# Adding the experts' output to a token-major stream: one-hot places, token weight on VectorE, last norm by token

## The chip, the cores and the metric

The kernel runs on one core of a Trainium2 chip. The metric is device time in microseconds (us) of one execution, median of several. Lower is better. In what follows PE is TensorE (matmuls), DVE is VectorE, ACT is ScalarE, POOL is GpSimd, SP is the engine whose queue issues nearly all loads.

## What is computed

One inference step of a two-layer backbone over 128 context tokens and 128 latent tokens, model width 1024, all in fp32. Each layer: a modulated RMS norm, attention and a pooling mixer, a gated residual; then a modulated RMS norm and a feed-forward part, dense in layer 0 and top-2-of-8 experts in layer 1, with a gated residual. A last RMS norm gives the two outputs. The change lies in the experts' part of layer 1 and in the last norm:

```
gates = sum(one_hot(top_i, 8) * softmax(top_v)[..., None], axis=1)
y = 0
for e in range(8):
    y = y + gates[:, e:e + 1] * swiglu(x, we_gate[e], we_up[e], we_down[e])
x = x + g2 * y                      # g2: one gate vector for the context tokens, one for the latents
out = x * rsqrt(mean(x * x) + EPS) * final_norm_g
```

## The kernel before

Five engines run programs written by hand, each in its own order, tied by semaphores. The residual stream is `xT`: channels on the 128 partitions (8 groups `k`), the 256 tokens (`b` = 0 context, 1 latents) along the free axis. The weights (466 MB in all) stream through a ring of slots that SP fills; a slot is filled again when the matmuls that read it have been counted in `pieces_used`.

**Routing.** After the last norm of layer 1, PE computes the router's logits (L1531), turns the normed activations to `h2` with tokens on partitions (L1535), and DVE picks the top two and each token's place among the tokens of its expert. `place` (L1148, L1152) writes two matrices for each expert: `P`, one-hot (token to one of CAP = 96 places), and `Pg`, the same with the token's weight in it. `gather(e)` (L1553) multiplies `h2` by `P` and gives `xg`, the expert's tokens with channels on partitions. PE transposes all `Pg` (L1586) to `PgT` before the first expert; ACT and DVE copy it out of PSUM.

**An expert.** Its 3584 hidden columns come in four steps. `gate_up` (L1610) multiplies the tokens with the gate and up weights; ACT applies silu (L845, L846), DVE multiplies (`hm`, L1203, L1204), PE transposes the result (`turn`, L1622), ACT and DVE copy it (`hT_first`, `hT_last`), and `down` (L1636) accumulates the expert's output in PSUM banks 3 to 5. Down matmuls of one step are interleaved with gate and up matmuls of the next. The expert's output leaves PSUM while the next expert's first step runs: ACT copies the even half to `Y` (`take_Y`), DVE adds the odd half (`add_Y`, L1177, L1182).

**The seam.** So at the end of each expert's first gate/up step PE does, in this order, the last expert's `combine` (L1565, eight products of `Y` and `PgT`, 256 columns each, in fp32, into banks 3, 4, 5 and 0), `turn(0)`, and then waits for `acc_ready`: DVE adds the four banks into an accumulator `acc` (`add_up`, L1189) that lies in the buffer called `sq`. The first matmul of step 1 writes where these results stood, so it comes behind the fourth addition. On DVE the two `hm` products of step 0 stand ahead of the four additions. The place is called the seam below; there are eight. At the first one PE and DVE add zeros.

```
                        if i + 1 == GATE_UP_END[0]:
                            pe.wait_ge(Y_ready, k + (rnd + 1))
                            combine(e, k * NSTEP + 1)
                            turn(0)
                            pe.wait_ge(acc_ready, k * 4 + (4 * rnd + 4))
```

**The end.** Every expert gathers for the next one before its last down matmuls, the eighth too, though nothing uses that. Then come `add_Y`, `combine` and `add_up` for the last expert, a register load and a branch (a second round of experts that these inputs don't need), 16 gated residual updates of `xT` on DVE (`residual`, L960), squares on ACT (L669), 16 sums over channels by one-column matmuls (L1265), root and reciprocal, a broadcast by matmul (L1273), eight scaled products on DVE (L909), 16 transposes (L1680), four copies and two stores of 512 KB.

Of the kernel before, what the change touches and what calls it, by code (L numbers as in the profile page):

```python
# [18 lines left out]
D = 1024  # L19
T = 128  # L20
DEPTH = 2
# [12 lines left out]
NE = 8  # L34
FE = 3584
EPS = 1e-6
# [29 lines left out]
        (0, 1, 0, 4, 0), (0, 1, 1, 4, 1), (1, 0, 2, 4, 2), (1, 0, 1, 4, 3),  # L66
        (1, 0, 0, 5, 0), (1, 1, 1, 5, 1), (1, 1, 2, 5, 2), (1, 1, 0, 5, 3))
TURN_BANK, GATHER_BANK = 6, 0
COMBINE_BANKS = (3, 4, 5, 0)
# [190 lines left out]
def program(nc, ins, consts, y_prompt, y_sample, new_ckv, new_kpe):  # L260
# [10 lines left out]
    with ctx:  # L271
# [35 lines left out]
        oh = sb("oh", 128, 4, 2, NE)  # L307
        over = sb("over", 128, 1, dt=i32)
# [54 lines left out]
        P = sb("P", 128, NE + 1, 2, CAP)  # L363
        PgT = sb("PgT", 128, NE + 1, 2, 128)
        Y = sb("Y", 128, D)
        xg = sb("xg", 128, KD, CAP)
        hT_first = sb("hT_first", 128, 4, 128)
        hT_last = sb("hT_last", 128, 4, 64)
        sg_at = place_at[0]
        sg = sb("sg", 128, 2, 512)  # L370
        hm = sb("hm", 128, 2, 512)

        place_at[0] = sg_at
        Pg = sb("Pg", 128, NE, 2, CAP)
        place_at[0] = sg_at + 4 * 2048
        yout = h2[:, :, :].rearrange("p b d -> p (b d)")
        acc = sq
# [26 lines left out]
        P_ready, Pg_ready, PgT_done, PgT_first_ready, PgT_last_ready = (sem(x) for x in ("P_ready", "Pg_ready", "PgT_done", "PgT_first_ready", "PgT_last_ready"))  # L404
        moe_zero, over_ready, shift_ready = sem("moe_zero"), sem("over_ready"), sem("shift_ready")
        esg_ready, eh_ready, ehT_done, ehT_first_ready, ehT_last_ready = (sem(x) for x in ("esg_ready", "eh_ready", "ehT_done", "ehT_first_ready", "ehT_last_ready"))
        Y_even_ready, Y_moved, Y_ready, cmb_done, acc_ready = sem("Y_even_ready"), sem("Y_moved"), sem("Y_ready"), sem("cmb_done"), sem("acc_ready")
        gat_done, xg_first_ready, xg_last_ready = sem("gat_done"), sem("xg_first_ready"), sem("xg_last_ready")
        outT_done, y_first_ready, y_second_ready = (sem(x) for x in ("outT_done", "y_first_ready", "y_second_ready"))
# [69 lines left out]
        def _(sp):  # L479
# [100 lines left out]
            sp.wait_ge(y_first_ready, 1)  # L580
            sp.wait_ge(y_second_ready, 1)
            sp.dma_start(y_prompt, yout[:, 0:D]).then_inc(stored, 16)
            sp.wait_ge(y_first_ready, 2)
            sp.wait_ge(y_second_ready, 2)
            sp.dma_start(y_sample, yout[:, D:2 * D]).then_inc(stored, 16)
# [5 lines left out]
        def _(pool):  # L591
# [40 lines left out]
        def _(act):  # L632
# [73 lines left out]
            def mixer(l):  # L706
# [75 lines left out]
                for m in gap[1:2]:  # L782
                    take_rows(m)
# [46 lines left out]
            def experts(rnd):  # L830
# [22 lines left out]
                with act.Fori(0, NE) as e:  # L853
                    expert(e)
# [853 lines left out]
```

## Time and profile before

| | |
|---|---|
| median of three runs | 1539.85 us (1538.51 to 1541.7) |
| the profiled execution | 1541.1 us |
| its span, first to last instruction | 1538.9 us |
| PE busy | 1467.5 us, 95% of the span |
| DVE busy | 365.6 us, 24% |
| ACT busy | 268.8 us, 17% |
| read from HBM | 462.80 MB, 302 GB/s over the span |
| mean granted clock of PE | 0.968 of 2.4 GHz |

The profiled execution's time is its span and 2.2 us around it. A busy share is an average over stages: the eight experts take about 120.7 us each, from about 538 us on, and what an engine's wait is worth there is read in one expert and counted eight times. The tail begins at 1504 us, when the last down matmul ends. The granted clock has two levels, 1.0 (2.4 GHz) and 0.5 (1.2 GHz); a value between is a mean over a stretch.

### The profile page before, as it was taken

The numbers are of one execution on the slowest core, as the hardware profiler recorded it, in microseconds if no ns is written. First come the engines' busy times: TensorE is split into PE (matmuls) and PEld (weight loads), VectorE is DVE, ScalarE is ACT, GpSimd is POOL, SyncE is SP. The second block draws the span as 40 slices with busy tenths as digits, with TensorE's granted clock in tenths as the row PEclk, the third lists the DMA queues.
The fourth block names the chain that finished last, engine by engine and source line by source line (L and its number), as shares of the span: only waits on it lengthen the run. The fifth ranks groups of instructions, "written<-read, shape, count | busy, mean of one in ns | idle before, by whom it ended". The sixth has DMA issues, their size and how long they took to land.

```text
span 1538.9 us, 29578 instructions
## 1 busy us (share of the span) xinstructions
PE 1467.5 (95%) x13084; PEld 798.5 (52%) x13084; DVE 365.6 (24%) x647; ACT 268.8 (17%) x434; POOL 30.9 (2%) x63
## 2 busy tenths in 40 slices
PE   5898999999998799999999999999999999999995
PEld 3857799998857733433343343343343343343344
DVE  2434555454433420020020011011011011002004
ACT  3323544443332300000000000000000000010001
POOL 0020000000020000000000000000000000000000
PEclk9899899998999699999999999999999999999997
DMA  9668877553663889989999999999999999999910
GB/s 346 223 226 297 290 263 249 188 181 124 222 226 114 328 294 393 385 323 378 396 347 357 394 351 354 391 353 347 398 354 345 391 361 346 386 364 351 378 73 29
DMA packets 164779, 466.05 MB, mean 303 GB/s; under 512 B 12810, under 2 KB 55476, under 8 KB 150324
## 3 DMA queue, kind: packets, MB, share of 16 engines
q1 hardware_dynamic: 162756, 462.81, 81.1%
q8 instruction: 104, 1.70, 0.4%
q10 hardware_dynamic: 1904, 1.41, 0.3%
q14 instruction: 15, 0.12, 0.0%
HBM read 462.80 MB, written 1.38 MB: 302 GB/s over the span
## 4 chain that ended last, share of the span: by engine, by line
PE 90%; DVE 4%; issue 2%; ACT 2%; SPq 1%; DMA 1%; DVEq 0%; ACTq 0%
PE ps L1610 38%; PE ps L1636 19%; PE ps L1326 5%; PE ps L1328 5%; PE ps L1327 5%; PE ps L1287 2%; PE ps L1553 2%; PE ps L1337 2%; PE ps L1622 2%; PE ps L1265 1%; PE ps L1499 1%; PE ps L1501 1%; PE ps L1500 1%; DVE sq L1189 1%; DMA ring<-in_w_ada 1%
## 5 line engine op out<-in xcount | busy, mean ns | idle before, releaser
L1610 PE MATMUL ps<-ering,xg 128*32 128x512 f32 (+1 forms) x6144 | 596.9, 539 | 4.9 <-DVE sq L1189 3.5
L1610 PEld LDWEIGHTS ps<-ering,xg 128*32 128x32 f32 x6144 | 198.4, 110 | 383.6 <-issue 347.6
L1636 PE MATMUL ps<-ering,hT_first 128*32 128x512 f32 x1792 | 307.6, 593 | 0.0
L1326 PE MATMUL ps<-hx,high 128*128 128x256 f32 x640 | 183.0, 286 | 16.8 <-DVE low L885 13.2
L1203 DVE TENSOR_TENSOR hm<-sg,ps 128x512 f32<-128x512 f32 (+1 forms) x32 | 19.9, 621 | 742.4 <-ACT sg L846 742.4
L1327 PE MATMUL ps<-hx,high 128*128 128x256 f32 x640 | 181.1, 283 | 0.0
L1328 PE MATMUL ps<-hx,low 128*128 128x256 f32 x640 | 181.0, 283 | 0.0
L1636 PEld LDWEIGHTS ps<-ering,hT_first 128*32 128x32 f32 x1792 | 82.1, 110 | 183.3 <-issue 177.1
L1636 PE MATMUL ps<-ering,hT_last 128*32 128x512 f32 x896 | 153.7, 592 | 0.0
L845 ACT ACTIVATE sg<-ps 128x512 f32<-128x512 f32 (+1 forms) x32 | 17.4, 544 | 748.0 <-PE ps L1610 748.0
L885 DVE TENSOR_TENSOR low<-ring,high 128x1024 fp32r<-128x1024 f32 x102 | 121.9, 1223 | 95.8 <-ACT high L653 95.8
L1326 PEld LDWEIGHTS ps<-hx,high 128*128 128x128 f32 x640 | 123.0, 192 | 21.5 <-DVE low L885 14.6
L1328 PEld LDWEIGHTS ps<-hx,low 128*128 128x128 f32 x640 | 123.0, 192 | 0.0
L1327 PEld LDWEIGHTS ps<-hx,high 128*128 128x128 f32 x640 | 122.6, 192 | 0.0
L653 ACT ACTIVATE high<-ring 128x1024 fp32r<-128x1024 f32 x102 | 104.3, 1055 | 73.8 <-PE ps L1328 39.9
L1287 PE MATMUL ps<-ring,silu_c 128*32 128x512 f32 x384 | 53.2, 680 | 0.1
L1499 PE MATMUL ps<-fx,high 128*128 128x256 f32 x176 | 49.5, 281 | 0.0
L1500 PE MATMUL ps<-fx,high 128*128 128x256 f32 x176 | 49.1, 279 | 0.0
L1501 PE MATMUL ps<-fx,low 128*128 128x256 f32 x176 | 49.1, 279 | 0.0
L1565 PE MATMUL ps<-PgT,Y 96*128 96x256 f32 x144 | 36.9, 413 | 6.2 <-DVE Y L1182 6.2
L1622 PEld LDWEIGHTS ps<-cst,hm 128*128 128x128 f32 x224 | 29.9, 207 | 22.3 <-DVE hm L1204 21.9
L1636 PEld LDWEIGHTS ps<-ering,hT_last 128*32 128x32 f32 x896 | 40.7, 110 | 0.0
(195 smaller groups left out, 942.9 us busy)
## 6 DMA issues: line engine op xcount, KB each, us to landing
ering<-in_moe_w_gate SPq DMA_DIRECT2D x224, 512.0 KB, 5.1
ering<-in_moe_w_up SPq DMA_DIRECT2D x224, 512.0 KB, 6.5
ering<-in_moe_w_down SPq DMA_DIRECT2D x112, 1024.0 KB, 7.2
ring<-in_w_ada SPq DMA_DIRECT2D x48, 1024.0 KB, 7.1
ring<-in_ffn_w_gate SPq DMA_DIRECT2D x11, 1024.0 KB, 5.6
ring<-in_ffn_w_up SPq DMA_DIRECT2D x11, 1024.0 KB, 7.4
ring<-in_ffn_w_down SPq DMA_DIRECT2D x11, 1024.0 KB, 5.5
ring<-in_w_in SPq DMA_DIRECT2D x8, 1024.0 KB, 9.4
```

The lines of the kernel that those rows point to most:

```text
L653: A(next(halves(q, raw)), raw, ACT.Copy).then_inc(high_ready, 1)
L885: V.tensor_tensor(lo, raw, hi, ALU.subtract).then_inc(low_ready, 1)
L1287: last = mm(mod_rows_of(m)[32 * i:32 * i + 32, :], silu_c[:, k, :], w[:, i, :], start=half == 0, stop=half == 1)
L1326: mm(out, hi[:, k, :], xh, start=n == 0, stop=False)
L1327: mm(out, hi[:, k, :], xl, start=False, stop=False)
L1328: last = mm(out, lo[:, k, :], xh, start=False, stop=n == KD - 1)
L1499: mm(o, hi[:, 0, mc], xh, start=a, stop=False, skip_group_check=True)
L1500: mm(o, hi[:, 0, mc], xl, start=False, stop=False, skip_group_check=True)
L1501: last = mm(o, lo[:, 0, mc], xh, start=False, stop=z, skip_group_check=True)
L1610: last = mm(ps[32 * group:32 * group + 32, bank, 0:width], xg[:, kk, 32 * g:32 * g + 32], w[:, t, r, c * width:(c + 1) * width], start=kk ...
L1622: last = nc.tensor.transpose(ps[:, TURN_BANK + part, n * 128:(n + 1) * 128], hm[:, part, a:a + 255:2], ident)
L1636: last = mm(ps[32 * group:32 * group + 32, bank, :], h, w[:, odd, 512 * half:512 * (half + 1)], start=(s, i) == (0, 0), stop=(s, i) == (NS ...
```

## The change

- **Stream.** Before layer 1's router PE transposes `xT` (between the sums of the norm, in `norm(3)`) and ACT and DVE copy it to `xt`, tokens on partitions. PE also broadcasts the gate vector g2 over all partitions (16 products of a broadcast column with the identity) into `gate`, which takes the place of `xT`.
- **Places.** Only the one-hot `P` is made. It is transposed to `PT` not before the first expert but in the middle of its first gate/up step (`turn_places`). The weights go to `w_slot`.
- **Output.** `take_Y` and `add_Y` keep the expert's output in `Y` and split it in `Yh` (rounded to the one-pass format `f32r`) and `Yl` (the rest). `combine` is now eight products of 512 columns, places times `Yh` and places times `Yl`, one pass each, four banks of tokens x channels.
- **Adding.** `add_up` takes two DVE instructions for each bank: `scalar_tensor_tensor` (PSUM times the token's weight times `gate`) into `gated`, then an addition to `xt` that waits for the first. PE waits for the fourth `gated_ready`.
- **First and last.** The first expert has no `add_Y`, `combine` or `add_up`; the last has no `gather`.
- **End.** `combine` for the last expert works half by half as `Yh` and `Yl` come. The norm is done with tokens on partitions: ACT squares and sums rows of `xt` in one instruction, then root, reciprocal and one product with `fin` (the last norm's gain, loaded over all partitions by a DMA on ACT's queue in the routing stage). No matmul of the norm and no transposes are left.

```diff
+COMBINE = ((0, 0, 3), (0, 1, 4), (1, 0, 5), (1, 1, 0))
+COMBINE_END = ((0, 0, 0), (0, 1, 1), (1, 0, 2), (1, 1, 6))
...
@@ gpsimd
             pool.wait_ge(h2T_done, 1)
-            nc.gpsimd.memset(P[:, NE, :, :], 0.0)
-            nc.gpsimd.memset(PgT[:, 0, :, :], 0.0)
-            nc.gpsimd.memset(hm[:, 1, :], 0.0)
-            nc.gpsimd.memset(acc[:, :, :], 0.0).then_inc(moe_zero, 1)
+            nc.gpsimd.memset(hm[:, 1, :], 0.0).then_inc(moe_zero, 1)
@@ scalar
+            act.dma_start(fin[:, :], ins["final_norm_g"].rearrange("(o n) -> o n", o=1).to_broadcast([128, D])).then_inc(fin_in, 16)
...
+            def take_Y(n, even=Y_even_ready, added=Y_ready, high_half=Yh_ready):
+
+
+                A(Y[0:CAP, 0:512], ps[0:CAP, 3, :], ACT.Copy).then_inc(even, 1)
+                A(Y[64:CAP, 512:1024], ps[96:128, 3, :], ACT.Copy).then_inc(even, 1)
+                A(Y[0:64, 512:1024], ps[0:64, 5, :], ACT.Copy).then_inc(even, 1)
+                for half in range(2):
+                    act.wait_ge(added, 2 * n - 1 + half)
+                    A(Yh[0:CAP, 512 * half:512 * (half + 1)], Y[0:CAP, 512 * half:512 * (half + 1)], ACT.Copy).then_inc(high_half, 1)
...
+            take_Y(1, Y_even_end, Y_end, Yh_end)
 
             for b in range(2):
-                A(yout[:, b * D:b * D + 512], ps[:, 1 + 2 * b, :], ACT.Copy).then_inc(y_first_ready, 1)
+                for half in range(2):
+                    act.wait_ge(xt_end, 2 * b + half + 1)
+                    A(squared_x[:, half, :], xt[:, b, 512 * half:512 * (half + 1)], ACT.Square,
+                      accum_out=stat[:, 2 * b + half:2 * b + half + 1]).then_inc(yss_ready, 1)
+                act.wait_ge(yrt_ready, 2 * b + 1)
+                A(rt[:, b:b + 1], rt[:, b:b + 1], ACT.Sqrt, scale=1.0 / D).then_inc(yrt_ready, 1)
@@ vector
-            def add_up(done):
-                for r, bank in enumerate(COMBINE_BANKS):
-                    dve.wait_ge(cmb_done, done + (r + 1))
-                    a = acc[:, 2 * r:2 * r + 2, :]
-                    V.tensor_tensor(a, a, ps[:, bank, :].rearrange("p (k t) -> p k t", k=2), ALU.add).then_inc(acc_ready, 1)
+            def add_Y(e, n, even=Y_even_ready, added=Y_ready, high_half=Yh_ready, low_half=Yl_ready, now=now_ready):
+
+
+                places = PT[0:CAP, e, :, :] if isinstance(e, int) else PT[0:CAP, bass.ds(e, 1), :, :].rearrange("p o b t -> p (o b) t")
+                V.tensor_copy(PT_now[0:CAP, :, :], places).then_inc(now, 1)
+
+                def odd(a, z, half, bank, at):
+                    y = Y[a:z, 512 * half:512 * (half + 1)]
+                    return V.tensor_tensor(y, ps[at:at + z - a, bank, :], y, ALU.add)
+
+                def low_of(half):
+                    x = slice(512 * half, 512 * (half + 1))
+                    dve.wait_ge(high_half, 2 * n - 1 + half)
+                    V.tensor_tensor(Yl[0:CAP, x], Y[0:CAP, x], Yh[0:CAP, x], ALU.subtract).then_inc(low_half, 1)
+
+                dve.wait_ge(even, 3 * n - 2)
+                odd(0, CAP, 0, 4, 0).then_inc(added, 1)
+                dve.wait_ge(even, 3 * n - 1)
+                odd(64, CAP, 1, 4, 96)
+                low_of(0)
+                dve.wait_ge(even, 3 * n)
+                odd(0, 64, 1, 5, 64).then_inc(added, 1)
+                low_of(1)
+
+            def add_up(e, n, combined=cmb_done, weighted=gated_ready, summed=xt_added, places=COMBINE):
+
+
+                for r, (b, half, bank) in enumerate(places):
+                    x = slice(512 * half, 512 * (half + 1))
+                    w = w_slot[:, b, e:e + 1] if isinstance(e, int) else w_slot[:, b, bass.ds(e, 1)]
+                    dve.wait_ge(combined, 4 * n - 3 + r)
+                    V.scalar_tensor_tensor(gated[:, r % 2, :], ps[:, bank, :], w, gate[:, b, x], ALU.mult, ALU.mult).then_inc(weighted, 1)
+                    dve.wait_ge(weighted, 4 * n - 3 + r)
+                    V.tensor_tensor(xt[:, b, x], xt[:, b, x], gated[:, r % 2, :], ALU.add).then_inc(summed, 1)
...
@@ tensor
+                    if t == 2 * DEPTH - 1:
+                        for b in range(2):
+                            last = nc.tensor.transpose(ps[:, X_BANK[b, k // 4], k % 4 * 128:(k % 4 + 1) * 128], xT[:, k, b * T:(b + 1) * T], ident)
...
             mixer(1)
+
+            pe.wait_ge(mod_ready, DEPTH * ADA_ITEMS)
+            for i, ((b, half), bank) in enumerate(GATE_BANK.items()):
+                if bank == 0:
+                    pe.wait_ge(normed, 2 * (2 * DEPTH - 1) + 2)
+                for k in range(4 * half, 4 * half + 4):
+                    row = mod[:, 1, 40 + k, b:b + 1].to_broadcast([128, 128])
+                    last = mm(ps[:, bank, k % 4 * 128:(k % 4 + 1) * 128], row, ident, start=True, stop=True)
+                if i % 2:
+                    last.then_inc(gate_done, 1)
...
+                for r, (b, half, bank) in enumerate(places):
+                    if hidden is not None and bank == 0:
                         pe.wait_ge(eh_ready, hidden)
+                    for part, (y, ready) in enumerate(zip((Yh, Yl), halves_of_Y)):
+                        pe.wait_ge(ready, 2 * n - 1 + half)
+                        last = mm(ps[:, bank, :], PT_now[0:CAP, b, :], y[0:CAP, 512 * half:512 * (half + 1)], start=part == 0, stop=part == 1)
+                    last.then_inc(combined, 1)
...
+                        if begins and i + 1 == GATE_UP_END[0] // 2:
+                            turn_places()
                         if i + 1 == GATE_UP_END[0]:
-                            pe.wait_ge(Y_ready, k + (rnd + 1))
-                            combine(e, k * NSTEP + 1)
+                            if begins:
+                                pe.wait_ge(PT_first_ready, rnd + 1)
+                                pe.wait_ge(PT_last_ready, rnd + 1)
+                            else:
+                                combine(k, k * NSTEP + 1)
                             turn(0)
-                            pe.wait_ge(acc_ready, k * 4 + (4 * rnd + 4))
+                            if not begins:
+                                pe.wait_ge(gated_ready, 4 * k)
                         elif what == "d" and s < NSTEP - 1 and j == 2 * E_WIDTH[s] // 256 - 1:
                             turn(s + 1)
-                            if s + 1 == NSTEP - 1:
+                            if s + 1 == NSTEP - 1 and not ends:
                                 gather(e + 1)
```

DVE at the seam, before: the two `hm` products, the first of four like additions into `acc` (`sq`), and the copy of the transposed hidden values behind them.

```order
L1203 TENSOR_TENSOR hm<-sg,ps 128x512 [waits esg_ready]
L1204 TENSOR_TENSOR hm<-sg,ps 64x512
L1187 REGISTER_ALU
L1189 TENSOR_TENSOR sq<-sq,ps 128x512 [waits cmb_done]
...
L1207 REGISTER_ALU
L1209 COPY hT_last<-ps 128x256 [waits ehT_done]
```

The same place now, with two of the four pairs (`sq` is where `gated` lies, `xT` where `gate` lies):

```order
L1267 TENSOR_TENSOR hm<-sg,ps 128x512 [waits esg_ready]
L1268 TENSOR_TENSOR hm<-sg,ps 64x512
L1246 SCALAR_TENSOR_TENSOR sq<-ps,w_slot,xT 128x512 [waits cmb_done]
L1248 TENSOR_TENSOR xt<-xt,sq 128x512 [waits gated_ready]
L1246 SCALAR_TENSOR_TENSOR sq<-ps,w_slot,xT 128x512 [waits cmb_done]
L1248 TENSOR_TENSOR xt<-xt,sq 128x512 [waits gated_ready]
...
L1273 COPY hT_last<-ps 128x256 [waits ehT_done]
```

Between the `hm` products and the fourth `gated_ready`, for which PE waits, four instructions have become seven, three of them behind a wait for the one ahead.

DVE in the tail, before, from the last `add_Y` on:

```order
L1182 TENSOR_TENSOR Y<-ps,Y 32x512 [waits Y_moved]
L1182 TENSOR_TENSOR Y<-ps,Y 32x512 x5
L1189 TENSOR_TENSOR sq<-sq,ps 128x512 [waits cmb_done] x4
L1221 UNCONDITIONAL_BRANCH [waits acc_ready]
L960 SCALAR_TENSOR_TENSOR xT<-sq,mod,xT 128x128 x16
L900 TENSOR_SCALAR rt<-ps 128x2 [waits ss_done,x_ready]
L902 RECIPROCAL rt<-rt 128x2 [waits rt_ready]
L909 SCALAR_TENSOR_TENSOR sq<-xT,vecT,ps 128x256 [waits rs_done]
L909 SCALAR_TENSOR_TENSOR sq<-xT,vecT,ps 128x256 x7
```

And now, `add_Y` and the first of the four pairs of `add_up`, and behind these the end for one of the two halves of the tokens:

```order
L1223 TENSOR_TENSOR Y<-ps,Y 96x512 [waits Y_even_end]
L1223 TENSOR_TENSOR Y<-ps,Y 32x512 [waits Y_even_end]
L1228 TENSOR_TENSOR Yl<-Y,Yh 96x512 [waits Yh_end]
L1223 TENSOR_TENSOR Y<-ps,Y 64x512 [waits Y_even_end]
L1228 TENSOR_TENSOR Yl<-Y,Yh 96x512 [waits Yh_end]
L1246 SCALAR_TENSOR_TENSOR sq<-ps,w_slot,xT 128x512 [waits cmb_end]
L1248 TENSOR_TENSOR xt<-xt,sq 128x512 [waits gated_end]
...
L1293 TENSOR_SCALAR rt<-stat 128x1 [waits yss_ready,fin_in]
L1295 RECIPROCAL rt<-rt 128x1 [waits yrt_ready]
L1297 SCALAR_TENSOR_TENSOR h_77<-xt,rt,fin 128x1024 [waits yrs_ready]
```

The 16 residual updates, the eight scaled products and the copies have gone from the tail; the branch now stands ahead of `add_Y`.

## Rows read from the trace of the kernel before

**Rows 1.** The page, part 5, whole span

```profile
L885 DVE TENSOR_TENSOR low<-ring,high 128x1024 fp32r<-128x1024 f32 x102 | 121.9, 1223 | 95.8 <-ACT high L653 95.8
```

**Rows 2.** Windows, one expert: stretch, length, busy by engine, granted clock, DMA, GB/s

```profile
1021.68:1142.40 120.72, 120.20 (x1185) 45.65 (x1180) 14.31 (x24) 7.59 (x15) 0.00 (x0) 1.00 0.96 366
```

**Rows 3.** Timeline of PE, one seam; columns: start, length, instructions [idle before]

```profile
1042.21 3.82 PE L1565 MATMUL ps<-PgT,Y 96*128 96x256 f32 x16
1045.87 1.11 PE L1622 MATMUL ps<-cst,hm 128*128 128x128 f32 x8
1047.41 5.36 PE L1610 MATMUL ps<-ering,xg 128*32 128x512 f32 x48 [0.44 <-DVE sq L1189]
```

**Rows 4.** Timeline of DVE, the same seam

```profile
1044.16 0.69 DVE L1204 TENSOR_TENSOR hm<-sg,ps 64x512 f32<-64x512 f32 x1
1044.88 2.48 DVE L1189 TENSOR_TENSOR sq<-sq,ps 128x512 f32<-128x512 f32 x4
```

**Rows 5.** Groups of DVE by shape, 500 to 1539: busy us, mean ns, idle before

```profile
L1189 DVE TENSOR_TENSOR sq<-sq,ps 128x512 f32<-128x512 f32 x36 | 22.6, 683 | 4.6 <-PE ps L1565 4.4
...
L960 DVE SCALAR_TENSOR_TENSOR xT<-sq,mod,xT 128x128 f32<-128x128 f32 x16 | 4.3, 344 | 1.2 <-issue 1.2
...
L909 DVE SCALAR_TENSOR_TENSOR sq<-xT,vecT,ps 128x256 f32<-128x256 f32 x8 | 3.2, 476 | 1.3 <-PE ps L1273 1.3
```

**Rows 6.** Timeline, all engines, from the last gather to the end

```profile
1495.55 3.71 PE L1553 MATMUL ps<-P,h 128*128 128x96 f32 x32
...
1504.62 0.59 ACT L827 ACTIVATE Y<-ps 96x512 f32<-96x512 f32 x1 [4.83 <-PE ps L1636]
...
1505.72 0.70 DVE L1177 COPY Y<-ps 32x512 f32<-32x512 f32 x1 [5.86 <-ACT Y L828]
1506.45 4.20 DVE L1182 TENSOR_TENSOR Y<-ps,Y 32x512 f32<-32x512 f32 x6
...
1510.70 6.34 PE L1565 MATMUL ps<-PgT,Y 96*128 96x256 f32 x16 [6.15 <-DVE Y L1182]
...
1518.97 4.29 DVE L960 SCALAR_TENSOR_TENSOR xT<-sq,mod,xT 128x128 f32<-128x128 f32 x16 [1.19 <-issue]
1520.14 0.63 ACT L669 ACTIVATE sq<-xT 128x512 f32<-128x512 f32 x1 [14.45 <-DVE xT L960]
...
1520.82 6.99 PE L1265 MATMUL ps<-ones,sq 128*128 128x1 f32 x32 [3.78 <-ACT sq L669]
...
1530.37 3.28 PE L1680 MATMUL ps<-cst,sq 128*128 128x128 f32 x16 [0.58 <-DVE sq L909]
...
1535.06 0.34 SPq L585 DMA_DIRECT2D out<-h  x1
```

**Rows 7.** Windows, tail and first gather; after POOL's column: the granted clock

```profile
1509.00:1510.00 1.00, 0.00 (x0) 0.00 (x0) 0.97 (x3) 0.00 (x0) 0.00 (x0) 0.61 0.00 0
...
1516.00:1517.00 1.00, 1.00 (x5) 0.59 (x3) 0.69 (x1) 0.00 (x0) 0.00 (x0) 0.98 0.00 0
...
1519.00:1520.00 1.00, 0.00 (x0) 0.00 (x0) 1.00 (x4) 0.00 (x0) 0.00 (x0) 0.73 0.03 8
...
1533.00:1534.00 1.00, 0.65 (x5) 0.41 (x4) 0.36 (x2) 0.31 (x1) 0.00 (x0) 0.94 0.00 0
...
528.50:534.50 6.00, 5.92 (x32) 5.78 (x32) 6.00 (x30) 0.01 (x1) 0.00 (x0) 0.62 1.02 412
```

**Rows 8.** Timeline, routing stage and start of the first expert

```profile
514.55 7.00 PE L1531 MATMUL ps<-wr,sq 128*128 128x8 f32 x32 [4.62 <-DVE sq L922]
...
528.54 5.92 PE L1553 MATMUL ps<-P,h 128*128 128x96 f32 x32 [1.55 <-DVE P L1148]
530.82 3.92 DVE L1152 TENSOR_SCALAR Pg<-cst,oh 128x96 f32<-128x96 f32 x16
...
535.25 1.95 PE L1586 MATMUL ps<-cst,Pg 128*96 128x128 f32 x16 [0.79 <-DVE over L1166]
...
538.62 20.81 PE L1610 MATMUL ps<-ering,xg 128*32 128x512 f32 x192 [1.42 <-ACT PgT L835]
```

More of the change, by code:

```diff
@@ L783, in mixer @@
                     take_rows(m)
+                if l:
+                    act.wait_ge(xt_done, 1)
+                    for b, half in ((0, 0), (1, 0), (0, 1)):
+                        A(xt[:, b, 512 * half:512 * (half + 1)], ps[:, X_BANK[b, half], :], ACT.Copy).then_inc(xt_first_ready, 1)
                 norm_b(2 * l + 1, l == 0)
@@ L806, in _ @@
             mixer(1)
+            act.wait_ge(gate_done, 2)
+            for b, half in ((0, 0), (1, 1)):
+                A(gate[:, b, 512 * half:512 * (half + 1)], ps[:, GATE_BANK[b, half], :], ACT.Copy).then_inc(gate_first_ready, 1)
             act.wait_ge(top2_ready, 1)
@@ L1191, in experts @@
             def experts(rnd):
+                if rnd:
+                    add_Y(NE, NE * rnd)
+                    add_up(NE, NE * rnd)
                 place(rnd)
@@ L1204, in expert @@
                         V.tensor_tensor(hm[0:64, 1, 0:width], sg[0:64, 1, 0:width], ps[64:128, 2, 0:width], ALU.mult).then_inc(eh_ready, 1)
-                        if s == 0:
-                            add_up(k * 4 + 4 * rnd)
+                        if s == 0 and not begins:
+                            add_up(e, k)
                         dve.wait_ge(ehT_done, k * NSTEP + (s + 1))
@@ L1209, in expert @@
                         V.tensor_copy(hT_last[:, 0:n, :], ps[:, TURN_BANK + 1, 0:width].rearrange("p (n t) -> p n t", n=n)[:, :, 0:64]).then_inc(ehT_last_ready, 1)
-                    take_xg(k + (rnd + 2))
-                with dve.Fori(0, NE) as e:
+                    if not ends:
+                        take_xg(k + 2)
+                expert(0, begins=True)
+                with dve.Fori(1, NE - 1) as e:
                     expert(e)
-                add_Y(9 * (rnd + 1))
-                add_up(36 * rnd + 32)
-                dve.wait_ge(acc_ready, 36 * (rnd + 1))
+                expert(NE - 1, ends=True)
             experts(0)
@@ L1673, in _ @@
                     experts(rnd)
-            norm(2 * DEPTH)
-            spread(2 * DEPTH)
-            for k in range(KD):
-                pe.wait_ge(h_ready, 2 * DEPTH + k + 1)
-                for b in range(2):
-                    last = nc.tensor.transpose(ps[:, 1 + 2 * b + k // 4, (k % 4) * 128:(k % 4 + 1) * 128], hT[:, k, b * T:(b + 1) * T], ident)
-            last.then_inc(outT_done, 1)
+            combine(1, None, now_end, (Yh_end, Yl_end), cmb_end, COMBINE_END)
 OVER_LIMIT = float(CAP)
```

198 lines of the change are left out of this document (107 added, 91 removed).

## Prediction

> **What bounds the kernel now.** I read one expert by windows first [rows 2]: PE is busy 120.20 of 120.72 us at the full clock, so almost all that an expert costs is PE's own work. The loads are not the bound: at 366 GB/s no matmul waits for them there, while the same queues gave 412 GB/s in the first gather [rows 7]. So PE time at the seam and in the tail counts in full, and longer DVE work counts where PE waits for it. The seam decides that [rows 3, 4]. PE begins `combine` at 1042.21 and gate/up of step 1 at 1047.41, that is 5.20 us, with a wait of 0.44 us for L1189 at the end. DVE starts the second `hm` product at 1044.16, ends it at 1044.85, and its four additions end at 1047.36: PE goes on 0.05 us later. So the seam ends by DVE today, and combine and turn lie beside it. The tail [rows 6] runs from the last down matmul (1504.55, by ACT's start) to 1538.9, 34.35 us, in a chain that goes from engine to engine.
>
> **The seam, seven times.** The cheaper `combine` (two passes for each bank in place of four) shortens PE work that DVE's chain covers, and is worth nothing. DVE's chain gets longer. One `scalar_tensor_tensor` takes 344 ns for 128 elements and 476 for 256 [rows 5], 132 for each 128 more, so 740 for 512. The addition of two SBUF tensors: L885 takes 1223 ns for 1024 [rows 1], less 533 (512 elements at the slope that these lengths give) is 690. The wait between the two costs what the wait between L1177 and L1182 does: start to start 0.73 for 0.70, so 0.03 [rows 6]. Behind an instruction that it needn't wait for, the next one starts early: four L1189 in 2.48 at 0.683 each [rows 4, 5] is a pitch of 0.60, 0.08 less than the length. A pair is then 0.74 + 0.03 + 0.69 - 0.08 = 1.38. The fourth `gated_ready` comes 3 x 1.38 + 0.74 = 4.88 us after 1044.88 where 2.48 stood: **+2.40 a seam, +16.8 for seven**. The `hT_last` copy queues behind it by 0.7 more, but its reader, `down`, comes two gate/up groups (5.36 in all [rows 3]) later. The copies to `PT_now`, `Yh` and `Yl` lie under the 20 us of gate/up. Bounds for a seam: -0.99 (DVE hidden, PE alone: `hm` end at 2.64, 0.43 for two products, 1.11 for the turn, 4.2 in all) and +2.9.
>
> The Trainium skill (VectorE: DVE Perf Modes, The DRAIN you can't avoid) says that the next instruction doesn't start before the pipe is empty and that a semaphore adds nothing. Here four additions overlap by 0.08 each. By that rule a pair would be 1.43 and the sum 1 us higher.
>
> **The clock at the seam.** This is the term I am least sure of. Now PE is without work from the end of `turn(0)` (1042.21 + 2.67 + 0.43 + 1.11 = 1046.4) to 1049.8: 3.4 us, and 1.4 us ahead of the fourth bank's products. In the tail the clock fell to half when PE had been idle from 1517.04 to 1519.46 (0.73 in that microsecond), 2.4 us, and another time only after 4.7 us, at 1509.2 [rows 6, 7]. 3.4 lies between. It rose after 4.6 us of gather (0.62 over 6 us from 528.5), after 5.3 us of `combine` (1510.70 to 1516.0), and 2.7 us after the transposes began at 1530.37 (0.94 in 1533 to 1534) [rows 6 to 8]. Work at half the clock loses half its time: 1.35 to 2.65, middle 2.0. Gate/up fills PE at the full clock [rows 2], so that loss is on the path. The first seam has an idle stretch of 2.7 too. I take seven of eight: **+14**; bounds 0 and 8 x 2.65 = 21.
>
> The Trainium skill (TensorE: Matmul & The Clock Gate, Part 4: PE-mode transpose) says that transposes don't count as work for the clock. Here it rose while PE did little but transposes [rows 6, 7]. By that rule the turn would count as idle, the gap would be 4.5, all eight seams would fall, and the sum would be 2 higher.
>
> **Start of the experts.** PE goes from the end of the gather (534.46) to gate/up at 538.62, 4.16 us, because Pg (3.92), its transposes (1.95) and the copies stand between [rows 8]. Now only the `xg` copy does, 0.6: -3.55. The 16 transposes come inside gate/up, 1.95 and about 0.25 for breaking the stream: +2.2. Ahead of it: 14 of 16 transposes at 0.12 in the norm delay its sums, at most 1.7. The 16 gate products lie in PE's 4.62 us idle stretch ahead of the router [rows 8] when the clock is full (16 x 0.22 = 3.5), and end up to 3 late at half clock; dense work there brings the clock up for part of the router's 7.0, which is at half (about 0.22 for each of 32, 0.12 at full). The `xt` and `gate` copies and POOL's shorter memsets cost nothing, hidden by the router; if the router were gone they would cost 2. The `fin` DMA delays ACT's `h2` copies by some 0.45, which the wait for P (1.55 [rows 8]) covers. I take -1.5 for it all, bounds -4 and +3. Together **-2.85**.
>
> **First seam.** Without `combine` and `add_up` it ends 2.64 + 0.05 + 1.11 = 3.8 after gate/up for 5.2: **-1.35**.
>
> **Last gather.** 3.71 us of PE [rows 6] go; the `hT` copies, so far beside it, show with 0.5: **-3.0** (bounds -3.6 and -2.5).
>
> **The tail**, from down's end as 0: three ACT copies (0.59 each, pitch 0.49) and the first odd addition, `Yh` at 2.2, `Yl` at 2.9, the other odd half 3.6, `Yh` 4.3, `Yl` 5.0 (ACT 0.63 in SBUF, DVE 0.69). Four pairs of 1.38 from 5.0: 10.6. Products are covered by these. Sum 0.16, root 0.20, reciprocal 0.17 with 0.03 between each, and a product of 1024 (0.74 + 0.53 = 1.27): the first half's output at 12.6. ACT squares the second half meanwhile (0.63 twice and the sum's read), and with the same steps it stands at 14.5. The last store: issue at 1535.06 to 1538.9 is 3.84 for two stores that share the queues; one alone of 512 KB at the 412 GB/s of [rows 7] is some 0.8 less, 3.1. End at 17.6 for 34.35: **-16.75** (bounds -18.5 and -14). Register load and branch, 1.19 ahead of L960 [rows 6], are hidden by the last down matmuls.
>
> **Sum.** +16.8 + 14 - 2.85 - 1.35 - 3.0 - 16.75 = +6.85. On the profiled execution's 1541.1 this is 1547.95. The median of the runs shown is 1.25 below that execution, so **1546.7**, +0.44%.
>
> **Rivals.**
> - *The clock stays up at the seams.* The stretch of 3.4 us is shorter than the 4.7 that it once took. Then the sum is -7.15: 1532.7, faster. Against it: the fall after 2.4. It decides as soon as the clock takes less than 7 us in all. Chance 0.16.
> - *It falls in about half of them, or rises soon*: +7, so 1539.7, no change. 0.20.
> - *It falls in all eight and stays down 5.3 us of work*: +21, so 1553.7. The Trainium skill's rule on transposes would lead here. 0.10.
> - *The change does what it says and DVE's pairs are covered*: -0.99 x 7, no clock loss, sum -31, 1509. It would need the pairs to fit in 1.5 us; nothing in the rows says so. 0.02.
> - *Forecast*, 1541 to 1551: 0.52.
>
> **Numbers.** 0.2% (3.1 us) is about what a measurement of this kernel can tell from no change. Faster: rival one, the fourth, and a little of the second, 0.19. Within: most of the second and the forecast's low end, 0.19. Slower: 0.62. The range for 8 in 10, 1534 to 1552, leaves out half of the first rival, the fourth and the upper half of the third; the likeliest case alone is 1541 to 1551.
>
> **What would show it.** Right: PE's wait at L1700 for `gated_ready` 3 us or more, seven times; the seam 7.6 us; a granted clock below 1.00 in expert windows, and an expert of 123 to 126 us. The tail from down's end to the end 17 to 19 us. Wrong: an expert of 123.1 with the clock at 1.00 (first rival); pairs on DVE shorter than 1.3; the gather ending later than 536, if the gate products are late.

## The result and the profile after

The changed kernel takes 1547.61 us (median of 8 runs, 1545.38 to 1550.56), the kernel before 1540.37 (8 runs, 1532.24 to 1544.3). The ratio is 1.0058, 95% interval 1.0042 to 1.0073: slower by 0.6%. The profiled execution of the changed kernel took 1548.21 us, its span is 1546.4, 7.5 more than before, and its mean granted clock 0.963 for 0.968.

The page of the changed kernel, first row of part 1, and the group of gate/up in part 5 (busy us, mean ns, idle time ahead and what ended most of it), with the same group of the kernel before behind it:

```profile
PE 1452.6 (94%) x12968; PEld 766.0 (50%) x12968; DVE 363.5 (24%) x624; ACT 283.7 (18%) x463; POOL 28.7 (2%) x60
...
L1700 PE MATMUL ps<-ering,xg 128*32 128x512 f32 (+1 forms) x6144 | 613.7, 551 | 23.5 <-DVE sq L1246 22.8
```

```profile
L1610 PE MATMUL ps<-ering,xg 128*32 128x512 f32 (+1 forms) x6144 | 596.9, 539 | 4.9 <-DVE sq L1189 3.5
```

PE is busy 15 us less than before in a span that is 7.5 us longer, so it is idle for 22.4 us more, and the group says behind what: DVE's L1246. The same 6144 gate/up matmuls are also busy for 613.7 us where they were for 596.9. The waits of PE from 500 us on (total us, times, longest):

```profile
PE ps L1700 <- DVE sq L1246: 22.8, 7, 3.3
PE ps L1654 <- DVE hm L1268: 7.2, 7, 1.0
...
PE ps L1712 <- DVE hm L1268: 2.8, 1, 2.8
```

Seven waits of 3.26 us at the seams are new; before, a seam had 0.44 [rows 3]. Two experts by windows (columns as in [rows 2]):

```profile
1029.52:1153.97 124.45, 120.06 (x1176) 43.68 (x1172) 16.16 (x27) 9.45 (x18) 0.00 (x0) 0.99 0.93 355
903.50:1029.52 126.02, 121.63 (x1177) 43.93 (x1172) 16.16 (x27) 9.44 (x18) 0.00 (x0) 0.97 0.92 351
```

An expert took 120.72 [rows 2]. Now it takes 124.45 or 126.02, and the clock is no longer 1.00. One seam on PE:

```profile
1050.05 0.50 PE L1654 MATMUL ps<-Yh,PT_now 96*128 96x512 f32 x1
...
1052.74 0.50 PE L1654 MATMUL ps<-Yh,PT_now 96*128 96x512 f32 x1 [1.04 <-DVE hm L1268]
...
1053.31 1.11 PE L1712 MATMUL ps<-cst,hm 128*128 128x128 f32 x8
1057.68 6.65 PE L1700 MATMUL ps<-ering,xg 128*32 128x512 f32 x48 [3.26 <-DVE sq L1246]
```

and on DVE:

```profile
1052.71 0.75 DVE L1246 SCALAR_TENSOR_TENSOR sq<-ps,w_slot,xT 128x512 f32<-128x512 f32 x1
1053.50 0.69 DVE L1248 TENSOR_TENSOR xt<-xt,sq 128x512 f32<-128x512 f32 x1
1054.11 0.74 DVE L1246 SCALAR_TENSOR_TENSOR sq<-ps,w_slot,xT 128x512 f32<-128x512 f32 x1
...
1056.88 0.74 DVE L1246 SCALAR_TENSOR_TENSOR sq<-ps,w_slot,xT 128x512 f32<-128x512 f32 x1
```

The fourth product ends at 1057.62, and PE goes on 0.06 later. From the first combine product (1050.05) to step 1 it is 7.63 us; before, 5.20. DVE's pairs follow each other at 1.39 (three pairs in 4.17, from 1052.71 to 1056.88).

Then the clock. These are the 48 gate/up matmuls that follow each of the eight seams (length, PE, weight loads, granted clock, DMA share, GB/s):

```profile
557.29:563.09 5.80, 5.80 (x48) 1.48 (x48) 0.89 0.24 54
681.07:687.94 6.87, 6.87 (x48) 1.81 (x48) 0.75 0.17 52
805.92:813.69 7.77, 7.77 (x48) 1.85 (x48) 0.66 0.15 44
931.67:939.71 8.04, 8.04 (x48) 1.86 (x48) 0.64 0.18 49
1057.68:1064.16 6.48, 6.48 (x48) 1.61 (x48) 0.79 0.15 42
1182.14:1189.54 7.40, 7.40 (x48) 1.78 (x48) 0.70 0.15 34
1307.50:1315.36 7.86, 7.86 (x48) 1.86 (x48) 0.65 0.16 42
1433.34:1441.43 8.09, 8.09 (x48) 1.86 (x48) 0.64 0.22 59
```

At the full clock such a stretch takes 5.17 (below, in the third experiment). The seven later ones are longer by 1.70, 2.60, 2.87, 1.31, 2.23, 2.69 and 2.92, in all 16.3 us; the first by 0.63.

The start of the experts on PE:

```profile
508.52 3.76 PE L1604 MATMUL ps<-cst,mod 128*128 128x128 f32 x32
513.31 3.74 PE L1614 MATMUL ps<-wr,sq 128*128 128x8 f32 x32 [1.02 <-DVE sq L958]
...
522.94 6.13 PE L1640 MATMUL ps<-P,h 128*128 128x96 f32 x32 [1.13 <-DVE P L1192]
529.77 10.51 PE L1700 MATMUL ps<-ering,xg 128*32 128x512 f32 x96 [0.70 <-ACT xg L845]
540.21 1.95 PE L1677 MATMUL ps<-cst,P 128*96 128x128 f32 x16
```

The router takes 3.74 for 7.00, and gate/up begins at 529.77 for 538.62 [rows 8]. The tail, all engines:

```profile
1528.34 0.59 ACT L850 ACTIVATE Y<-ps 96x512 f32<-96x512 f32 x1 [5.51 <-PE ps L1726]
...
1533.54 0.75 DVE L1246 SCALAR_TENSOR_TENSOR sq<-ps,w_slot,xT 128x512 f32<-128x512 f32 x1
...
1537.18 1.28 ACT L904 ACT_TABLE_LOAD   x1
...
1539.77 1.28 DVE L1297 SCALAR_TENSOR_TENSOR h<-xt,rt,fin 128x1024 f32<-128x1024 f32 x1
...
1541.65 1.28 DVE L1297 SCALAR_TENSOR_TENSOR h<-xt,rt,fin 128x1024 f32<-128x1024 f32 x1
```

It runs from 1528.28, the last down matmul's end, to 1546.4: 18.12 us for 34.35.

Both profiled executions, stage by stage:

| stage | before | after | difference |
|---|---|---|---|
| to the first sum of layer 1's second norm | 503.20 | 502.29 | -0.9 |
| from there to the first gate/up | 35.42 | 27.48 | -7.9 |
| turn of the places inside gate/up | 0 | 2.02 | +2.0 |
| first seam (last gate/up matmul to step 1) | 5.71 | 5.28 | -0.4 |
| seven seams, by the same measure | 7 x 5.72 | 7 x 8.16 | +17.1 |
| low clock behind eight seams | 0 | 16.95 | +16.95 |
| last expert from step 1 to the end of down, without the low clock's part | 94.98 | 92.02 | -3.0 |
| tail | 34.35 | 18.12 | -16.2 |
| sum | | | +7.6 |

The first row is partly chance: the part of the kernel up to that sum took 494.4 to 505.0 us in the fourteen profiles of this document, and these two executions happen to lie 0.9 apart.

### The profile page after: what moved, and what is told of

It reads as the page before. It is cut to its first block, busy times and chain, and to the rows that moved or that the text cites. A ratio compares the mean times of both kernels' runs of the same rounds, so it can differ in the third digit from the quotient of the medians.

```text
span 1546.4 us, 29377 instructions
## 1 busy us (share of the span) xinstructions
PE 1452.6 (94%) x12968; PEld 766.0 (50%) x12968; DVE 363.5 (24%) x624; ACT 283.7 (18%) x463; POOL 28.7 (2%) x60
## 3 DMA queue, kind: packets, MB, share of 16 engines
HBM read 463.33 MB, written 1.38 MB: 301 GB/s over the span
## 4 chain that ended last, share of the span: by engine, by line
PE 89%; DVE 6%; ACT 2%; issue 2%; DMA 0%; SPq 0%; DVEq 0%; ACTq 0%
PE ps L1700 39%; PE ps L1726 18%; PE ps L1399 5%; PE ps L1401 5%; PE ps L1400 5%; PE ps L1360 2%; PE ps L1640 2%; PE ps L1410 2%; PE ps L1712 2%; DVE sq L1246 2%; PE ps L1572 1%; PE ps L1574 1%; PE ps L1573 1%; PE ps L1332 1%; PE ps L1370 1%
## 5 line engine op out<-in xcount | busy, mean ns | idle before, releaser
L1700 PE MATMUL ps<-ering,xg 128*32 128x512 f32 (+1 forms) x6144 | 613.7, 551 | 23.5 <-DVE sq L1246 22.8
L1712 PE MATMUL ps<-cst,hm 128*128 128x128 f32 x224 | 35.3, 299 | 3.6 <-DVE hm L1268 2.8
```

What stands on the lines that cost most here:

```text
L1700: last = mm(ps[32 * group:32 * group + 32, bank, 0:width], xg[:, kk, 32 * g:32 * g + 32], w[:, t, r, c * width:(c + 1) * width], start=kk ...
L1712: last = nc.tensor.transpose(ps[:, TURN_BANK + part, n * 128:(n + 1) * 128], hm[:, part, a:a + 255:2], ident)
```

## Experiments

The two theories: (A) the seam costs twice, by DVE's longer chain and by the clock, which falls because PE waits; (B) the long gate/up stretches behind the seams have another cause than the wait (late weights, the shorter combine, the turn). Each kernel is timed against the kernel before on one chip; the chip differs between some of the runs, and a difference of two medians from two chips is uncertain by a few us.

**Idle products in the wait.** Between the turn and the wait for `gated_ready` stand products that nobody reads:

```diff
                             if not begins:
+                                for _ in range(14):
+                                    mm(ps[:, 1, :], PT_now[0:CAP, 0, :], Yh[0:CAP, 0:512], start=True, stop=True)
                                 pe.wait_ge(gated_ready, 4 * k)
```

> The changed kernel with 14 extra one-pass products (places times Yh, into bank 1, which step 1 overwrites) between the turn and the wait at each of the seven later seams; DVE's work is untouched. They take about 3.0 us of the 3.26 us that PE waits there. My theory (waiting and the clock are two costs, and the second is about 2.3 us a seam): the seam stays at 7.6 us, the granted clock stays at 1.00 through seven experts, the first gate/up group goes from 6.6 to 8.3 us back to 5.36, and the time falls by about 16, from 1547.6 to 1531 to 1532. Rival (the long first groups have another cause, such as weights that come late): the time stays within 2 us of the changed kernel or grows.

1529.08 us, ratio to before 0.9928 (0.9903 to 0.9952). A seam of this kernel:

```profile
1050.46 1.11 PE L1712 MATMUL ps<-cst,hm 128*128 128x128 f32 x8
1051.32 3.44 PE L1747 MATMUL ps<-Yh,PT_now 96*128 96x512 f32 x14
1054.84 5.36 PE L1700 MATMUL ps<-ering,xg 128*32 128x512 f32 x48
```

The seam is as long as ever (8.16), the wait is filled, and none of the seven stretches behind it is longer than 5.18. The seven stretches give 16.3 us back, the median 18.5 (against that of the first measurement, on another chip). The two profiled executions lie only 12.0 apart (1536.25 and 1548.21), because this one reached the first gate/up 2.85 us later and lost 1.47 more behind the first seam, where nothing was changed. So the clock's part is about what the rows said. The order of the loads, DVE's work, the turn and the length of the seam are what they were, and the long stretches are gone: late weights or the turn did not make them, PE's idle time did. Theory A stands; whether the shorter combine has a part is the question of the long combine below.

**Bank 0 first.** DVE's order is changed, and PE's wait is split:

```diff
-                for r, (b, half, bank) in enumerate(places):
+                order = (3, 0, 1, 2) if places == COMBINE else (0, 1, 2, 3)
+                for r, i in enumerate(order):
+                    b, half, bank = places[i]
...
@@ down
                         if i == 0:
+                            if s == 0 and not begins:
+                                pe.wait_ge(gated_ready, 4 * k)
...
@@ seam
-                                pe.wait_ge(gated_ready, 4 * k)
+                                pe.wait_ge(gated_ready, 4 * k - 3)
```

> The changed kernel with DVE taking bank 0 first in add_up (order 0, 3, 4, 5), PE waiting for the first product only before gate/up of step 1, and for the fourth before the first down product, two gate/up groups later. My theory: PE waits for bank 0 alone, the seam is PE's own turn plus a short wait, 4.2 to 4.6 us for 7.6, the clock does not fall there, and the time falls by 7 x 3.2 + 16 = 38, to about 1509 to 1513. Rival 1 (the clock falls whatever the wait, because the turn and the hm wait alone are enough): 1524 to 1527. Rival 2 (DVE's chain, which still takes 5.5 us, makes the hT_last copy late for the first down product): a new wait of 1 to 2 us a seam at that product, 1517 to 1525.

1505.31 us, ratio 0.9777 (0.9755 to 0.9798). The seam on PE:

```profile
1032.12 0.50 PE L1656 MATMUL ps<-Yh,PT_now 96*128 96x512 f32 x1 [1.04 <-DVE hm L1270]
...
1032.70 1.11 PE L1714 MATMUL ps<-cst,hm 128*128 128x128 f32 x8
1033.82 5.36 PE L1702 MATMUL ps<-ering,xg 128*32 128x512 f32 x48
```

From 1029.43, the first combine product, to 1033.82 it is 4.39 for 7.63. Step 1 follows the turn without a wait. The clock stays at 1.00 through the seven experts. Only bank 0 is written by step 1; banks 3 to 5 are needed by `down`, two gate/up groups later. There DVE's longer queue shows a little:

```profile
1037.19 0.74 DVE L1248 SCALAR_TENSOR_TENSOR sq<-ps,w_slot,xT 128x512 f32<-128x512 f32 x1
...
1038.58 0.42 DVE L1275 COPY hT_last<-ps 128x256 f32<-128x256 f32 x1
1039.14 1.45 PE L1730 MATMUL ps<-ering,hT_first 128*32 128x512 f32 x9
```

The fourth product ends at 1037.93, but the `hT_last` copy only at 1039.00, and the first down matmul begins 0.14 behind it, 5.32 after step 1 for 5.17. So rival 1 of this run is out, and rival 2 is right in kind: it costs 0.15 a seam, 1 us in all, where it named 1 to 2 a seam. The time is 4 us below the range that I gave; a second measurement below lies in it.

**Four products first**, then the four additions, with four buffers for `gated`:

```diff
-                    dve.wait_ge(weighted, 4 * n - 3 + r)
-                    V.tensor_tensor(xt[:, b, x], xt[:, b, x], gated[:, r % 2, :], ALU.add).then_inc(summed, 1)
+                for r, (b, half, bank) in enumerate(places):
+                    dve.wait_ge(weighted, 4 * n - 3 + r)
+                    V.tensor_tensor(xt[:, b, x], xt[:, b, x], gated[:, r, :], ALU.add).then_inc(summed, 1)
```

> The changed kernel with the four scalar_tensor_tensor of a seam first, in four buffers, and the four additions behind them; PE waits for the fourth product as before. My theory: the fourth product comes 4 x 0.66 after the hm products, the seam is 5.2 to 5.5 us, PE is idle only 1.2 us ahead of step 1, the clock stays up, and the time falls by 7 x 2.2 + 16 = 31, to about 1516 (1513 to 1520). Rival (the clock falls at a wait of any length there): 1532. Rival 2 (the DVE queue as a whole sets the seam, not the fourth product): no change.

1516.81 us, ratio 0.9859 (0.9834 to 0.9885). DVE at a seam:

```profile
1034.59 2.73 DVE L1247 SCALAR_TENSOR_TENSOR sq<-ps,w_slot,xT 128x512 f32<-128x512 f32 x4
1037.23 2.49 DVE L1255 TENSOR_TENSOR xt<-xt,sq 128x512 f32<-128x512 f32 x4
```

The time lies in the range that I gave. The fourth product ends 2.73 after the first begins, the seam is 5.97 for 8.16 by the table's measure, and PE's wait ahead of step 1 is 1.07. I expected the clock to stay up. It did at five of seven seams, and fell at two. One stretch of 48 gate/up matmuls of each kind:

```profile
672.92:678.09 5.17, 5.17 (x48) 1.46 (x48) 1.00 0.25 63
1037.37:1044.24 6.87, 6.87 (x48) 1.81 (x48) 0.75 0.23 60
```

**Six idle products** where the first run had 14:

> The changed kernel with 6 extra products at the seam for the 14 of the earlier run: 1.3 us of the 3.26 us are filled, about 2.0 us stay idle. The seam stays at 7.6 us. In the kernel with its four scalar_tensor_tensor first, 1.07 us of idle time there let the clock fall at 2 of 7 seams. My theory (each idle microsecond raises the number of seams at which the clock falls): 2 to 5 of seven fall, 1534 to 1542. Rival (any filling keeps the clock up): 1531.

1534.66 us, ratio 0.9961 (0.9943 to 0.9979). The wait is 1.88, and the clock fell at two of seven seams, with 3.4 us in all. By the sums of the stretches it should stand 16.3 - 3.4 = 12.9 below the changed kernel: 1534.7. That the median meets this to 0.1 is chance, since the stretches are of one execution (it took 1538.35) and the medians of two chips.

**A combine as long as before.** The first product of each bank is made three times:

```diff
+                        if part == 0 and places == COMBINE:
+                            for _ in range(2):
+                                mm(ps[:, bank, :], PT_now[0:CAP, b, :], y[0:CAP, 512 * half:512 * (half + 1)], start=True, stop=True)
```

> The changed kernel with the first of the two products of each bank made three times over, so that PE has 16 passes in combine, as in the kernel before, for 8; DVE's work and all waits are untouched, and PE is still idle for about 2.8 us of the 3.26 us before step 1. My theory (the idle stretch itself brings the clock down): it still falls in most of the seven seams, and the time is 0 to 6 us below the changed kernel, 1542 to 1548. Rival (the clock falls because combine became short, the wait alone would not do it): all seven first gate/up groups back at 5.36, 1531 to 1533.

1540.89 us, ratio 1.0007 (0.999 to 1.0025). The wait ahead of step 1 is 2.74, and the wait for `hm` within combine is gone. The clock fell at five of seven seams, with 9.4 us in all, and the time lies 1.1 below the range that I gave and far above the rival's. So the wait alone does bring the clock down. The long combine takes 1.03 + 0.52 us of idle time away and puts work there; which of the two saved the clock at the other two seams, this run can't tell. The kernels in one table (idle time ahead of step 1 and ahead of the fourth bank's products, and the seven stretches, from one profile of each):

| kernel | wait ahead of step 1 | wait for `hm` within combine | long stretches of 7 | us lost in them | median |
|---|---|---|---|---|---|
| changed | 3.26 | 1.03 | 7 | 16.3 | 1547.6 |
| long combine | 2.74 | 0 | 5 | 9.4 | 1540.9 |
| 6 products | 1.88 | 1.03 | 2 | 3.4 | 1534.7 |
| four products first | 1.07 | 1.03 | 2 | 3.3 | 1516.8 |
| 14 products | 0.07 | 1.03 | 0 | 0 | 1529.1 |
| bank 0 first | 0 to 0.03 | 1.03 | 0 | 0 | 1505.3 |

**The kernel before with bank 0 first**, by a like edit to its own additions:

```diff
-                for r, bank in enumerate(COMBINE_BANKS):
+                for r in (3, 0, 1, 2):
+                    bank = COMBINE_BANKS[r]
...
-                            pe.wait_ge(acc_ready, k * 4 + (4 * rnd + 4))
+                            pe.wait_ge(acc_ready, k * 4 + (4 * rnd + 1))
```

> The kernel before with the same order of banks as the fast version of the changed kernel: DVE adds bank 0 first, PE waits for that addition before step 1 and for all four before the first down product. My theory (before, PE's own combine and turn are nearly as long as the seam): hm ends at 2.64, two products of the fourth bank 0.95, turn 1.11, so 4.7 us for 5.2, eight times 0.5: 4 us below the kernel before. Then most of the 33 us between the kernel before and that fast version come from the change once its wait is gone, and not from the order. Rival (the order alone gives the gain): 1515 or less.

1536.38 us, ratio 0.9988 (0.9973 to 1.0002). That doesn't part from no change by its time. Its profile shows the gain that was expected: the seam is 5.21 by the table's measure for 5.72, and the experts take 961.81 for 965.93, 4.1 less. But this edit changes the order in the tail as well, which the edit to the changed kernel leaves alone (`places == COMBINE`), and there it costs. The tail before, and now:

```profile
1510.70 6.34 PE L1565 MATMUL ps<-PgT,Y 96*128 96x256 f32 x16 [6.15 <-DVE Y L1182]
1512.82 0.69 DVE L1189 TENSOR_TENSOR sq<-sq,ps 128x512 f32<-128x512 f32 x1 [2.17 <-PE ps L1565]
...
1517.09 0.69 DVE L1189 TENSOR_TENSOR sq<-sq,ps 128x512 f32<-128x512 f32 x1 [0.18 <-PE ps L1565]
```

```profile
1498.12 7.06 PE L1566 MATMUL ps<-PgT,Y 96*128 96x256 f32 x16 [6.15 <-DVE Y L1182]
...
1505.22 2.48 DVE L1190 TENSOR_TENSOR sq<-sq,ps 128x512 f32<-128x512 f32 x4 [7.15 <-PE ps L1566]
```

All four additions now stand behind the fourth bank's products. From combine's start to the last addition's end it is 9.58 for 7.08, 2.5 more, of which combine itself has 0.7. So the time holds 4.1 us of gain at the seams and some 2 us of loss in the tail. At the seams the order alone is worth 4 us to the kernel before; behind the change it is worth about 40.

**The start: 16 idle products ahead of the router, in the kernel before.**

```diff
+            for i in range(16):
+                mm(ps[:, 7, i % 4 * 128:(i % 4 + 1) * 128], mod[:, 1, 40 + i % 8, 0:1].to_broadcast([128, 128]), ident, start=True, stop=True)
             pe.wait_ge(h_ready, 4)
```

> The kernel before with 16 idle products of 128 columns (a broadcast column times the identity, into a bank nobody reads) where PE waits for the activations ahead of the router; nothing else changed. My theory (the start gained about 8 us instead of 2.85 because the gate products keep PE's clock up, so that router, turn and gather run at full speed): router 3.8 for 7.0 us, the gather starts 3 to 5 us earlier, time 3 to 5 us below the kernel before, about 1536. Rival (the early start comes from the removed Pg work alone): no change, 1540.

1534.07 us, ratio 0.9973 (0.9952 to 0.9993), 4.15 below the kernel before. The products and the router:

```profile
505.77 5.37 PE L1526 MATMUL ps<-cst,mod 128*128 128x128 f32 x32
510.97 3.64 PE L1534 MATMUL ps<-wr,sq 128*128 128x8 f32 x32
```

The router takes 3.64 for 7.00 [rows 8]; in the profile of the kernel before with bank 0 first, whose start is unedited, it takes 7.00 too. So with PE's wait filled the clock is up for the router in this execution. That the gate products do the same in the changed kernel, and that part of its gain at the start is their by-product, was then my reading; the next run was to test it.

**Four of 16 gate products, in the changed kernel.** This kernel leaves out three quarters of the gate vectors.

```diff
-                for k in range(4 * half, 4 * half + 4):
+                for k in range(4 * half, 4 * half + 1):
                     row = mod[:, 1, 40 + k, b:b + 1].to_broadcast([128, 128])
```

> The changed kernel with 4 of the 16 gate products ahead of the router (one for each bank), so three quarters of the gate vectors are left out and the output does not hold the experts' part rightly. PE is idle 2.8 us longer there. My theory (those products keep the clock up, and that is what the start gained beyond my 2.85 us): the router takes 6 to 7 us for 3.7 and the gather starts 3 to 5 us later after the norm's sums; time 1 to 4 us above the changed kernel on the same chip. Rival (the start gained by the removed Pg work alone): the same or lower by up to 1 us.

1549.26 us, ratio 1.0077 (1.0053 to 1.0101), beside 1549.6 for the changed kernel on the same chip:

> The changed kernel again, unedited, as the measure for the three others of this chip: 1545 to 1550.

(1549.6 us, ratio 1.006, 1.0037 to 1.0083.) The kernel with four products:

```profile
502.03 0.83 PE L1604 MATMUL ps<-cst,mod 128*128 128x128 f32 x6
504.64 0.49 PE L1604 MATMUL ps<-cst,mod 128*128 128x128 f32 x2 [1.77 <-DVE sq L949]
506.81 6.12 PE L1614 MATMUL ps<-wr,sq 128*128 128x8 f32 x32 [1.69 <-DVE sq L958]
```

and the changed kernel in this second profile:

```profile
508.96 3.77 PE L1604 MATMUL ps<-cst,mod 128*128 128x128 f32 x32
513.75 6.12 PE L1614 MATMUL ps<-wr,sq 128*128 128x8 f32 x32 [1.02 <-DVE sq L958]
```

My expectation failed twice. The four products cut the idle time into pieces of 1.77 and 1.69, so the run didn't make the long idle stretch that it was meant to; and the router takes 6.12 in the unedited kernel too, for 3.74 in its first profile. Which of the two a run shows differs from execution to execution. The ten profiles of versions with all 16 gate products have the router at 3.69 to 4.05 in six and at 5.98 to 6.13 in four. In five of the six the gate products themselves ran partly at the low clock (4.34 to 5.04 for 3.76) and left PE idle for at most 0.48 ahead of the router; in the sixth, the first profile, and in all four slow ones they took 3.76 or 3.77 and PE was idle for 1.02. So the router was slow in four of the five executions with that idle time and in none of the others; why not in the fifth is open. From the first sum to the first gate/up the ten took 27.48 to 30.76, 29.5 in the mean, and the first profile has the lowest of them.

This second profile shows one thing more of the seams. Its stretches of 48 gate/up matmuls behind the seven later ones are 6.87, 7.82, 8.07, 6.50, 7.40, 7.86 and 8.09, and in the kernel with four products 6.87, 7.83, 8.08, 6.50, 7.40, 7.86 and 8.09: each within 0.06 of the same seam's in the first profile. So the clock fell at 21 of 21 seams of this kind, and that one seam loses 1.3 and another 2.9 is not chance but repeats. What sets it, no run here tells.

**Once more, and with the first seam filled.** The version with bank 0 first, and the same with 10 idle products (into bank 3) while the first expert's seam waits 2.81 us for `hm`:

```diff
                                 pe.wait_ge(PT_last_ready, rnd + 1)
+                                for _ in range(10):
+                                    mm(ps[:, 3, :], PT[0:CAP, 1, 0, :], PT[0:CAP, 1:3, :, :].rearrange("p e b t -> p (e b t)"), start=True, stop=True)
```

> The changed kernel with bank 0 first on DVE, as before, and 10 idle products at the first expert's seam while PE waits 2.8 us for hm, so that the clock stays up there too. My theory: the low stretch at about 551 us goes, 1.5 to 2 us less than the version without them, about 1503 to 1504. Rival (PE reaches the turn later because of the products): 1505 to 1506.

1508.61 us, ratio 0.9801 (0.9779 to 0.9822). I had expected 1503 to 1504, and it is above the 1505.31 of the version without them, measured on another chip, so both ran again side by side:

> The version with bank 0 first on DVE again, unedited, beside the changed kernel on one chip and beside the version with idle products at the first seam. My theory: 38 to 42 us below the changed kernel, 1505 to 1509. Rival (the 1505 of its first measurement was a lucky chip): 1512 or more.

> The same with 10 idle products at the first expert's seam, again. On another chip it read 3 us more than the version without them had on its own, though the low clock at the first seam was gone; in the profiles the difference came from the routing stage, before the first expert. My theory: on one chip the two differ by less than 3 us, with this one 1 to 2 us lower. Rival (the idle products cost time): 2 to 3 us higher again.

Without the idle products 1511.18 us, ratio 0.9822 (0.9801 to 0.9844), and with them 1511.14, ratio 0.9807 (0.9783 to 0.9831). The 38 to 42 us below the changed kernel that I expected of bank 0 first came out as 38.4, though its time lies 2 above the range beside them; the gain of 1 to 2 us by the idle products did not show. In the profiles the products do what they should: the first seam is 4.47 for 5.26, and the stretch behind it 5.17 for 6.00, 1.6 us in all. The first measurement of bank 0 first was 6 us lower than the second; in its profile the norm of layer 1 began 3.7 us earlier (496.22 for 499.87) and the routing stage was 1.5 shorter.

## Why the prediction was right

Slower was forecast, 1546.7 us, and 1547.6 was measured. The sum was +6.85 on the profiled execution, and the span grew by 7.5. The signs named for it came: seven waits of 3.26 us, a seam of 7.63, experts of 124.45 to 126.02, a tail of 18.12. Its terms one by one:

- **DVE's chain, +2.40 a seam, +16.8.** Measured 7.63 - 5.20 = 2.43, and 17.1 in the table. The pair was put at 1.38 and is 1.39. The four additions of the third experiment follow each other at 0.60 to 0.62 and its products at 0.66, so the overlap of 0.08 for an instruction that needn't wait holds for both kinds. The Trainium skill (VectorE: DVE Perf Modes, The DRAIN you can't avoid) says that the next instruction does not start before the pipe is empty, which would have made the pair 1.43, and adds that one which is not held starts earlier. The trace agrees with the addition, which the prediction left out, and not with 1.43.
- **The clock, +14.** Right in kind, low by 3. I took seven of eight seams at a mean of 2.0. It fell at all eight; a later seam lost 1.31 to 2.92 (bounds 1.35 to 2.65), mean 2.33, and the first 0.63. That seven of eight would fall was a choice between two idle times of the tail, 2.4 and 4.7 us; the clock then fell in runs with waits of 1.07 and 1.88 too. The third rival had the number of seams right and the price wrong: 5.3 us of work at the low clock would be +21, measured +17. The Trainium skill (TensorE: Matmul & The Clock Gate, Part 4: PE-mode transpose) says that transposes don't count as work for the clock. No run here can judge it: a wait of 3.26 us behind the turn brought the clock down in all seven seams whatever the turn counts for.
- **Start, -2.85.** In the first profile -5.9 (-7.9 and +2.0), in the second, with 30.74 for this stage, -2.7; with the mean of the ten, 29.5, it is -3.9. What I could not see is that the router runs at either level in executions of one kernel.
- **First seam, -1.35.** Measured -0.4. The low clock began ahead of the turn, which took 1.95 for 1.11, and the wait for `hm` was 2.81. I had charged the fall only to the work behind the seam.
- **Last gather, -3.0.** Measured -3.0, with the wait of 0.5 for the `hT` copies.
- **Tail, -16.75.** Measured -16.2. The new tail takes 18.1 in all eleven profiles that have it, the old one 33.4 and 34.35 in the two where it is unedited. ACT's copies out of PSUM follow each other at 0.61 where I took 0.49, and the four pairs began 5.3 after down's end for 5.0. A table load of 1.28 on ACT ahead of the root, which I did not have, is hidden by DVE's additions.

Two errors cancel: the clock took 3 more than I thought, and the start gave 3 more in that execution. The total is nearer than its parts, and that the profiled executions differ by 7.5 where the medians differ by 7.2 is luck too, with first stages that vary by 10 us. The mechanism does not rest on that: the waits at the seams, the clock behind them and the tail came out alike in three profiles.

## What to carry to other kernels

When a consumer's chain gets longer, look at which of its results the waiting engine needs next, and have that one made first: here one bank of four, and the same order that was worth 4 us at the seams before the change is worth 40 behind it. Where nothing waits early, as in the tail before, the same order costs. A wait of some microseconds on PE was paid twice here, once as time and once as half speed behind it; a first test is to fill the wait with products that nobody reads, which prices the second part without touching the first. Before a change in the routing or tail stages is judged by one profile, compare that stage in several executions.

## What the runs showed of the hardware

The clock fell after waits much shorter than the 2.4 us that I had seen in the tail: 1.07 us (with 1.03 some 1.7 us before it) was enough at 2 of 7 seams of one execution, and equal seams of the kernel with the long combine lost between 0 and 2.96 us. The 1.03 alone, with at most 0.07 ahead of step 1, lost nothing at any of 35 seams (the 14 products and four profiles of versions with bank 0 first). With 3.26 and 1.03 the clock fell at 21 of 21, and each seam lost the same to 0.06 us in three executions. The same router products, with the same idle time of 1.02 ahead of them, took 3.74 us in one execution of the changed kernel and 6.12 in another; in the ten profiles with all gate products that idle time stands five times, four of them with the slow router.
